# Attention maps divided before their transpose, and two heads per value product

## The reference

```python
# two first layers, three branches each: forget-gated (8 heads of 64), latent (8 of 96, values of 64),
# and a window of 128 keys with a sink logit per head (8 heads, 2 key heads: head h uses key head h // 4)
s = einsum('bqhd,bkhd->bhqk', qi, k) * scale       # + forget terms; masked
p = softmax(s, axis=-1)                            # window branch: over s and the sink's logit
o = einsum('bhqk,bkhd->bqhd', p, v)
branches = y * silu(z)                             # then w_branch, gates, w_out
# the later mixers: differential attention (4 heads, two maps each, values of 128), dilated attention
# (8 heads of 64), and latent attention over the 256 best keys of an index (16 heads, in two groups of 8)
```

## Time and profile before

| | |
|---|---|
| time, median of 3 runs | 2898.91 us (2895.21 to 2900.93) |
| span of the profiled execution (its only time in the profile) | 2914.3 us |
| mean granted clock of TensorE | 0.970 |
| busy: TensorE, VectorE, ScalarE | 2751.4, 1594.9, 1152.1 us |
| busy: weight loads of TensorE | 2329.2 us |
| DMA | 205.32 MB, mean 70 GB/s |

### The profile page before, as it was taken

The page is one execution under the profiler, slowest core; times in us unless marked ns, Lnnn a source line. Parts: engine busy times, 40 slices in busy tenths (PEclk is TensorE's granted clock), DMA queues, the critical chain, the costliest instruction groups (busy, mean ns, idle before and its releaser), DMA issues.

```text
span 2914.3 us, 39559 instructions
## 1 busy us (share of the span) xinstructions
PE 2751.4 (94%) x15260; PEld 2329.2 (80%) x15260; DVE 1594.9 (55%) x3412; ACT 1152.1 (40%) x2518; POOL 31.6 (1%) x32
## 2 busy tenths in 40 slices
PE   7999999999999999999998999999998689999998
PEld 7888889989888887877786777888775467788887
DVE  5454656555545565655578564343567844634446
ACT  3333432443323433343435453333345454432333
POOL 1000000000000000000000000000000000000000
PEclk9997999999999999999999999999998799999999
DMA  3201212212220121222321122323321001232322
GB/s 127 80 24 32 71 37 73 63 59 91 80 84 26 56 62 45 86 61 84 89 83 40 55 69 84 101 94 94 94 78 40 24 29 37 76 102 95 101 94 94
DMA packets 115260, 205.32 MB, mean 70 GB/s; under 512 B 13824, under 2 KB 23680, under 8 KB 114944
## 3 DMA queue, kind: packets, MB, share of 16 engines
q1 hardware_dynamic: 113920, 198.60, 22.6%
q10 hardware_dynamic: 1152, 4.20, 0.4%
HBM read 200.58 MB, written 2.10 MB: 70 GB/s over the span
## 4 chain that ended last, share of the span: by engine, by line
PE 79%; DVE 12%; ACT 7%; issue 2%; DMA 0%; DVEq 0%; ACTq 0%; SPq 0%
PE pp L2066 20%; PE pp L2068 19%; PE pp L2067 19%; PE pp L2138 5%; PE pp L2114 4%; PE pp L2126 2%; DVE wl L1632 2%; ACT wh L1445 1%; PE pp L2062 1%; PE pp L2063 1%; PE pp L2064 1%; ACT P L1561 1%; DVE P L1860 1%; PE pp L2086 1%; PE pp L2146 1%
## 5 line engine op out<-in xcount | busy, mean ns | idle before, releaser
L2066 PE MATMUL pp<-Hh,wh 128*128 128x512 f32 (+1 forms) x2304 | 860.4, 373 | 63.1 <-DVE wl L1632 24.4
L2068 PE MATMUL pp<-Hh,wl 128*128 128x512 f32 (+1 forms) x2304 | 797.7, 346 | 0.0
L2067 PE MATMUL pp<-Hl,wh 128*128 128x512 f32 (+1 forms) x2304 | 797.4, 346 | 0.0
L1632 DVE TENSOR_TENSOR wl<-raw,wh 128x512 fp32r<-128x512 f32 (+2 forms) x774 | 500.5, 671 | 461.9 <-ACT wh L1445 452.8
L1445 ACT ACTIVATE wh<-raw 128x512 fp32r<-128x512 f32 (+2 forms) x774 | 451.1, 605 | 344.8 <-PE pp L2068 290.1
L2066 PEld LDWEIGHTS pp<-Hh,wh 128*128 128x128 f32 x2304 | 445.0, 193 | 144.2 <-DVE wl L1632 30.6
L2067 PEld LDWEIGHTS pp<-Hl,wh 128*128 128x128 f32 x2304 | 445.5, 193 | 55.2 <-issue 7.0
L2068 PEld LDWEIGHTS pp<-Hh,wl 128*128 128x128 f32 x2304 | 443.6, 193 | 51.5
L2066 PE MATMUL pp<-Yh,wh 128*128 128x512 f32 (+1 forms) x1254 | 470.9, 376 | 3.8 <-DVE Yl L1652 2.0
L2068 PE MATMUL pp<-Yh,wl 128*128 128x512 f32 (+1 forms) x1254 | 448.6, 358 | 0.0
L2067 PE MATMUL pp<-Yl,wh 128*128 128x512 f32 (+1 forms) x1254 | 448.6, 358 | 0.0
(11 more groups left out here) (244 smaller groups left out, 2626.0 us busy)
## 6 DMA issues: line engine op xcount, KB each, us to landing
raw<-in_w SPq DMA_DIRECT2D x698, 256.0 KB, 2.6
raw<-in_w SPq DMA_DIRECT2D x36, 192.0 KB, 2.4
raw<-in_w SPq DMA_DIRECT2D x40, 128.0 KB, 2.0
out<-X SPq DMA_DIRECT2D x8, 256.0 KB, 2.0
con<-in_con ACTq DMA_DIRECT2D x1, 1576.0 KB, 11.7
X<-in_x SPq DMA_DIRECT2D x2, 528.0 KB, 5.9
X<-in_x ACTq DMA_DIRECT2D x2, 528.0 KB, 7.0
Z<-in_p ACTq DMA_DIRECT2D x2, 512.0 KB, 3.2
```

The lines of the kernel that those rows point to most:

```text
L1632: e.tensor_tensor(part("wl", j), landing(j), part("wh", j).bitcast(F), ALU.subtract).then_inc(*dve.up("split", j))
L2066: e.matmul(it.ps, wh, xh, start=it.first, stop=False)
L2067: e.matmul(it.ps, wh, xl, start=False, stop=False)
L2068: e.matmul(it.ps, wl, xh, start=False, stop=it.end).then_inc(*pe.up())
```

## The change

A new function `attend_pairs` writes all stages but the differential one, which keeps `attend`. In it

- each map is divided by its sum before the transpose: VectorE takes the reciprocal of one column (and adds the sink), ScalarE multiplies the map in place (`divide map`). The exp has its own `do` after `turn`, and the division of a unit comes at the beginning of the next iteration that has new scores;
- the transposed maps of two heads lie side by side in `PT` (chunk, head, 128 queries), and `pair product` takes 128 columns of `V` (two heads' values) as the stationary operand and moves the 256 columns of both maps. The output is the transposed output: rows 0 to 63 of its first 128 columns belong to one head, rows 64 to 127 of the last 128 to the other;
- so outputs are not divided and not transposed (`divided` and its `turn_out` go); `times_z` or `parts` read the two halves from bank 6 after every pair, eight instructions for eight heads in place of one;
- in the window branch the pairs are heads h and h + 4, and the gate's columns and the rows of `w_branch` are ordered to match.

Fill slices are spread over 2(n + 4) places for n units, before 2(n + 3) + 3. The counts of score products, of transposes of maps and of weight products stay.

```diff
-    def attend(heads, finish, steps, total, banks=2, slots=None, tail=None, turned_by=("dve", "act")):
+    def attend_pairs(heads, finish, steps, total, banks=2, slots=None, turned_by=("dve", "act")):
...
+        now = mark()
+        paired = slots is not None
...
+            n = u["n"] = units["n"]
+            units["n"] += 1
+            qr, ext = u["qr"], u["ext"]
+            assert u.get("after") != []
+            slot, bk, cut = n % len(slots), n % banks, max(0, ext - 512)
+            [(q, k)] = u["qk"]
+            p = u["p"] = slots[slot][0:qr, 0:ext]
...
+        def exp(u):
+            do("exp", u=u["n"], maps=[u["map"]], sink=u.get("sink"))
+
+        def divide(u):
+            do("divide map", u=u["n"], p=u["p"], sum=u["sums"][0], extra=u["sink"][1] if "sink" in u else None)
+
+        def turn(u, x):
+            whole = [c for c in u["chunks"] if c[1] == 128]
+            small = [c for c in u["chunks"] if c[1] != 128]
+            n = u["n"]
+            by = u["by"] = turned_by[x]
+            do("turn", u=n, qr=u["qr"], p=u["p"], exp=("act", "map", n), small=small[0][0] if small else None, whole=[c[0] for c in whole],
+               free5=free[5], free4=free[4], pt_free=pt_free["at"], ident=ident, b4=bank(4), b5=bank(5),
+               pt=pt[:, 0:len(whole), x, :], pt_small=pt[:, 4, x, :], by=by)
+            if small:
+                free[5] = ("dve", "turned small", n)
+            if whole:
+                free[4] = (by, "turned", n)
+            pfree[u["slot"]] = ("pe", "turn", n)
+
+        def product(a, b):
+            c = a["pair"]
+            small = [(4, v) for _, rows, v in a["chunks"] if rows != 128]
+            whole = [(x, v) for x, (_, v) in enumerate([(o, v) for o, rows, v in a["chunks"] if rows == 128])]
+            n = do("pair product", us=(a["n"], b["n"]), by=(a["by"], b["by"]), out=bank(6)[:, 0:256],
+                   pt=[(pt[:, x, :, :], v) for x, v in small + whole], vready=a["vready"], free=free[6], small=bool(small), whole=bool(whole))["n"]
+            pt_free["at"] = ("pe", "pair product", n)
+            free[6] = finish(a, c, bank(6)[:, 0:256], ("pe", "pair product", n))
+
+        rot["banks"] = [3, 7] if banks == 3 else FILL
+        last = None
+        for n in range(len(heads) + deep + 2):
+            new = []
+            if n < len(heads):
+                new = heads[n:n + 1] if not paired else heads[n:n + 2] if n % 2 == 0 else []
+            if last and (new or n >= len(heads)):
+                for u in last:
+                    divide(u)
+                last = None
+            for u in new:
+                scores(u)
+            fill()
+            if len(ready) == 2:
+                product(*ready)
+                ready.clear()
+            if n >= deep and scored:
+                u = scored.pop(0)
+                turn(u, len(ready))
+                ready.append(u)
+            for u in new:
+                exp(u)
+            scored += new
+            last = new or last
+            fill()
+        assert not ready and not scored and not last
+        run(steps)
+        rot["banks"] = FREE
+
...
         def product(u):
...
-    def divided(u, t, e1=None, alle=None):
-        qr = u["qr"]
-        n = do("divide", sums=u["all"], o=m["O"][0:qr, :].rearrange("p (h d) -> p h d", h=8), alle=alle, e1=e1,
-               ps=bank(6)[0:qr, :].rearrange("p (h d) -> p h d", h=8), qr=qr, t=t, turned=turned["o"])["n"]
-        free[6] = ("dve", "divide", n)
-        return free[6]
-
     X = v3("X", T, 8)
     do("load", X=m["X"], con=con, sm=sm, k1=k1)
 
...
-        def zgate_steps(c0, c):
+            zgate(c0, c, **fields)
+
+        def zgate_steps(c0, c, apart=False):
             def evac(ps, a, b, t):
                 n = do("zgate", ps=ps, zz=tmp[:, 0, 0:b - a], g=tmp[:, 1, 0:b - a], rs=rs[:, a:b], dst=Z[:, c, a:b], t=t, turned=tmp_turned["at"])["n"]
                 return ("dve", "evac", n)
-            yield from win(cols(c0 + 128 * c, 128), QR, evac)
+            yield from win([*cols(c0 + 64 * c, 64), *cols(c0 + 64 * (c + 4), 64)] if apart else cols(c0 + 128 * c, 128), QR, evac)
 
...
         def finish_to(n):
-            def finish(u, t):
+            def finish(u, c, ps, t):
                 qr, a = u["out"], u["tok"]
-                r = divided(u, t, ("act", "sink", u["n"]) if "sink" in u else None, u["alle"] if "sink" in u else None)
-                yield
-                yield
-                x = turn_out(128, r)
                 q = tmp[:, 0, 0:4 * qr].rearrange("p (c n) -> p c n", c=4)
-                f = do("times_z", q=q, ps=bank(5)[:, :].rearrange("p (c n) -> p c n", c=4)[:, :, 0:qr], z=Z[:, :, a:a + qr], t=x,
-                       turned=tmp_turned["at"])["n"]
-                free[5] = ("dve", "evac", f)
-                tmp_turned["at"] = parts(q, *(y[:, :, a:a + qr] for y in Yv[n % 2]), free[5])
+                f = do("times_z", q=q[:, c, :], ps=ps, qr=qr, z=Z[:, c, a:a + qr], t=t, turned=tmp_turned["at"] if c == 0 else None)["n"]
+                if c == 3:
+                    tmp_turned["at"] = parts(q, *(y[:, :, a:a + qr] for y in Yv[n % 2]), ("dve", "evac", f))
+                return ("dve", "evac", f)
             return finish
 
...
+                sums, e1 = st[0:qr, at:at + 8], st[0:qr, at + 8:at + 16]
+                for x, h in enumerate((0, 4, 1, 5, 2, 6, 3, 7) if window else range(8)):
                     q, k = qk(h)
                     u = dict(qr=qr, ext=ext, tok=a, mask=mk, scale=scale[i + 1] if isinstance(scale, list) else -scale, qk=[(q[:, a:a + qr], k[:, k0:k0 + ext])],
-                             chunks=[(o, r, vof(v, h)) for o, r, v in chunks], dv=64, out=NM if i < 0 else 128, o=64 * h,
-                             sums=[sums[:, h:h + 1]], all=sums, alle=e1, init=big[0:qr], ready=ready, head=headed.get(h), vready=vready)
+                             chunks=[(o, r, vof(v, x // 2)) for o, r, v in chunks], out=NM if i < 0 else 128, pair=x // 2,
+                             sums=[sums[:, x:x + 1]], init=big[0:qr], ready=ready, head=headed.get(h), vready=vready)
                     if sinks is not None:
                         u["init"], u["after"] = negs[0:qr, h:h + 1], ("dve", "negs", negd)
-                        u["sink"] = (sm[0:qr, sinks + h:sinks + h + 1], e1[:, h:h + 1])
-                    if h == 7:
-                        u["end"] = True
+                        u["sink"] = (sm[0:qr, sinks + h:sinks + h + 1], e1[:, x:x + 1])
                     us.append(u)
...
                 yield from win(cols(B0 + 128 * c, 128), TOKR, lambda ps, a, b, t, c=c: scaled(M[:, c, a:b], ps, rs[:, a:b], t, before))
-        attend(units_of(lambda h: (Q[0:66, h, :], K[0:66, h, :]), lambda v, h: V[:, v, 64 * h:64 * h + 64], 0.125, qk_ready, v_ready), finish_to(0), latent(), 80)
+        attend_pairs(units_of(lambda h: (Q[0:66, h, :], K[0:66, h, :]), lambda v, c: V[:, v, 128 * c:128 * c + 128], 0.125, qk_ready, v_ready), finish_to(0), latent(), 80)
...
     def finish2(y0):
-        def finish(u, t):
+        def finish(u, c, ps, t):
             a = u["tok"]
-            r = divided(u, t)
-            yield
-            yield
-            x = turn_out(128, r)
-            src = bank(5)[:, :].rearrange("p (c n) -> p c n", c=4)
-            free[5] = parts(src, Yh[:, y0:y0 + 4, a:a + 128], Yl[:, y0:y0 + 4, a:a + 128], x)
+            for x in range(2):
+                rows = slice(64 * x, 64 * x + 64)
+                f = parts(ps[rows, 128 * x:128 * x + 128], Yh[rows, y0 + c, a:a + 128], Yl[rows, y0 + c, a:a + 128], t)
+            return f
         return finish
 
...
-    def scores(it):
+    def exp(it):
         for x, p in enumerate(it.maps):
             act.wait_ge("dve", "scored", it.u, x)
             e.activation(p.p, p.p, AF.Exp, bias=p.neg, scale=-1.0, accum_out=p.sum).then_inc(*act.up("exp", it.u))
@@ -1563,13 +1625,17 @@
             sink, e1 = it.sink
             e.activation(e1, sink, AF.Exp, bias=it.maps[0].neg, scale=1.0).then_inc(*act.up("sink", it.u))
 
+    def divide_map(it):
+        act.wait_ge("dve", "factor", it.u)
+        e.activation(it.p, it.p, AF.Copy, scale=it.sum).then_inc(*act.up("map", it.u))
+
...
-    def divide(it):
-        if it.e1:
+            w = len(it.whole)
+            e.tensor_copy(it.pt, it.b4[:, 0:128 * w].rearrange("p (c n) -> p c n", c=w)).then_inc(*dve.up("turned", it.u))
+
+    def divide_map(it):
+        dve.wait_ge("act", "exp", it.u)
+        if it.extra is not None:
+            dve.wait_ge("act", "sink", it.u)
+            e.tensor_tensor(it.sum, it.sum, it.extra, ALU.add).then_inc(*dve.up())
             dve.wait_ge("dve")
-            dve.wait_ge(*it.t)
-            dve.wait_ge(*it.e1)
-            e.tensor_tensor(it.sums, it.sums, it.alle, ALU.add).then_inc(*dve.up())
-        dve.wait_ge("dve")
-        dve.wait_ge(*it.t)
-        e.reciprocal(it.sums, it.sums).then_inc(*dve.up())
-        dve.wait_ge("dve")
```

(36 more changed lines are left out.)

122 lines of the change are left out of this document (60 added, 62 removed).

## The result

| | |
|---|---|
| time after, median of 5 runs | 2916.93 us (2916.14 to 2921.83) |
| time before, median of 5 runs beside them | 2899.28 us (2895.21 to 2903.02) |
| ratio, 95% interval | 1.0059 (1.0042 to 1.0077) |
| span of the profiled execution, clock | 2914.3 us, 0.978 |

The change makes the kernel slower by 0.6%, some 17 us. The forecast was 2888 us and faster; the time lies inside the range, in the rival "the division is late" (2905 to 2927 us).

What follows compares the result with a forecast made beforehand. The prediction took TensorE to bound all stages but three VectorE-bound blocks of the selected attention. Its terms, -17 - 9 - 2 + 8 + 7 + 8 + 2 - 8, gave -11 us off the 2898.91 us median: 2888 us, range 2862 to 2918.

Steps and rivals of the forecast that it cites:

- the division is late: Rival: at each transpose TensorE waits for exp, reciprocal and division over two queues; 2905 to 2927 us, chance 0.22.
- What bounds the kernel: All stages: TensorE bounds, except three blocks of the selected attention, where VectorE is at 85% and TensorE at 71%.
- all this hides beside TensorE where TensorE is full: Map divisions: 168 us more of ScalarE, 50 us of reciprocals and 12 us of additions cost nothing where TensorE is full.
- Division of the maps: 312 maps: scaled copies on ScalarE, 168 us more, and reciprocals on VectorE, 50 us, hidden where TensorE is full.
- paired stages: Window and dilated stages, going by two units: late divisions stall 0.13 us a pair, 7 us more, bounds 0 and 16.
- with over 15 us there as the sign: Sign that the forecast is wrong: transposes of maps wait for the division for more than 15 us in sum.
- Transposes of outputs and their waits: Removed output transposes save 17 us, TensorE's waits for them and the gate 9, shorter chains at stage ends 2.
- The dilated stage: First blocks here and in the last stage: ScalarE's divisions and splits, 2 us more; pairs' late divisions share 7 us.
- Small evacuations elsewhere: Eight 64x128 evacuations replace one of 128x512; the added VectorE work is free where TensorE is full.
- The value product: Pair products on TensorE: 0.44 us a pair against 0.42 before, 420 times, 8 us more, bounds 3 and 21.
- Selected attention: Three blocks that VectorE bounds: more reciprocals and small evacuations, with waits for late exps 8 us more, bounds 5 and 25.
- The clock: First stage's last block: 27.3 us at half clock go with two removed stalls, 8 us less, bounds 0 and 14.

Runs made afterwards that it cites:

- late evacuation: Changed kernel with the evacuation of a pair's product issued after the next map's transpose and its copy, no longer ahead of them: 2909.93 us, ratio 1.0022.

## Why the prediction was wrong

**What bounds the kernel: right.** TensorE is the bound of most stages and VectorE of three blocks. But the step from there, "all this hides beside TensorE where TensorE is full", is the one that failed. A busy share of 57% for VectorE and 39% for ScalarE was read as room. It is room for work that nobody waits for at once; here the work came into two queues whose heads wait for each other, and behind the heads stand the copies that TensorE's next transpose and product need.

**Division of the maps.** Prices and counts were right within some 20 us (ScalarE 1318.6 us for some 1340, VectorE 1666.7 for 1690). What they cost was booked at 7 us in paired stages, at 2 us in first blocks and within the 8 us of the selected attention, 17 at the most, and measured at 28: 10 for the copies, 17 for the reciprocals. It fell in other places than booked. The dilated stage, with 16 of the 52 pairs, paid nothing for it. The first mixer paid 13.8 us: 6.4 in its window stages, near what was booked for them, and 7.4 in stages of single units, for which nothing was booked. The selected attention paid 9.9. The prediction named the mechanism as a rival that turns the sign at 0.035 us a map beyond what it took; 28 us over 312 maps are 0.09 in all, and 0.035 to 0.07 beyond the 7 to 17 us that it took. It expected the stall at the transposes' wait for the division, with over 15 us there as the sign. The direct waits are 7.5 us, and the copies queued behind wait 16 us more than without the division: the larger part of the stall was outside the row in which the sign was looked for.

**Transposes of outputs and their waits (-17, -9, -2).** Both are gone, as counted. The part of the change without the division gains 13 us by the medians, although its dilated stage is 10 us longer; so it gains some 23 us elsewhere, where the prediction has -28 and +8 for the product. Some of that may be clock (below).

**The dilated stage (+2, and a share of the 7 for pairs).** From it to the selected attention the changed kernel loses 9.5 us, and both terms looked for the loss in the wrong thing, the late division and ScalarE's load. Without division it is the same 10 us. What is left as the cause is the pairs: TensorE's waits for VectorE's copies of maps, which stand behind the small evacuations as at 1644.11, went from 2.2 us to 10. The late evacuation brought them down to 2.0, but the stage became only 2.8 us shorter, so the rest stays open.

**Small evacuations elsewhere (0).** The sum put them at nothing where TensorE is full; moving them behind the copy is worth some 11 us there.

**The value product (+8).** Right in mechanism, small in size: 0.215 us an instruction, so 0.43 us a pair against 0.42, and +4 us. The measured end was the bound that the trace gave by two cycles a column. The Trainium skill ("TensorE: Matmul & The Clock Gate", Back-to-back issue gap) gave 0.22 us by its gap taken twice for two passes; the trace agrees, with 0.215. (Taken without rounding, that estimate is 0.218 us an instruction and 0.44 a pair, so 7 us and not the 5 of the prediction.)

**Selected attention (+8).** The three blocks at 2266 went from 77.4 to 82.4 us and the whole first stage of that mixer by 6.9 us, a little under the 8. Without the division that stage is 3 us shorter than before: the loss is the division's, not that of the evacuations.

**The clock (-8).** This term failed in method. With its 27.3 us the stretch at half clock belonged to one long execution; the prediction took what its removal gives off the median of the runs, of which it was hardly a part. The span stood 15 us over the median, and that difference was the warning. The stalls named as its cause were not the mistake: the clock falls in the second of them in both executions of the kernel before, and in the changed kernel there is a new stall of 1.49 us at 210.5 and a stretch of 3.4 us at 211.6. What differs from one execution to the next is how long the clock stays down. Whether the change gained anything by the clock no run separates. The granted clock was 0.974 in the median of the 71 executions of the kernel before and 0.976 to 0.978 in the changed kernel, and the six executions of the kernel before at 0.977 or more took 5 to 9 us less than its median.

Put together: some -23 outside the dilated stage without the division, +10 in the dilated stage, +28 for the division, is +15, as measured against the median of 2901.9 us. The forecast had -20, +2, +15 and -8 for the clock. The first of these shares is the other two taken from the measured times, so the sum is no test of it. Why the stretches at half clock last as long as they do stays open.

## What to carry to other kernels

An engine's idle share is no cover for an instruction that sits between two in-order queues: ask what stands behind it in both while it waits, and look for the price at those, not at its own consumer. Moving work from the full engine pays only with its place in the order: the same evacuations cost 11 us more ahead of a copy than behind it, and the same reciprocals 69 us more behind the scores than ahead of them. Leave a suspect out and compare stage by stage before blaming it: the dilated stage lost 10 us with and without the division. Before a gain is taken off a median, check that the profiled execution is a median one.

## What the runs showed of the hardware

- A reciprocal of 128x1 on VectorE takes 161 ns, and the power of a 128x1 column on GpSimd 555 ns; a 128x1 addition takes 147 ns on VectorE and about 200 on GpSimd.
- Stretches at 1.2 GHz, half of the 2.4, begin at the same work in two executions of the same kernel and differ in length: 27.3 and 6.8 us behind the same two stalls, 20.5 and 51.2 us in the selected attention.
- A product of 256 moved f32 columns has a start every 0.215 us, one of 64 columns every 0.105 us beside its own weight load: 0.84 ns a column against a fixed 0.105 us. By these two the load of the stationary side and the columns would weigh the same near 125 columns, an estimate; no run here tried a width between.
